# A mixture-of-experts stage: experts with up to 32 rows get a body of their own, with groups of 32 columns

## The chip, the cores and the metric

The kernel runs on one core of a Trainium2 chip (trn2). The metric is the device time of one execution in microseconds (us), taken as the median of several runs.

## What is computed

The program is a transformer-like block of several layers on 256 tokens of width 1024, all in fp32. The change lies in its mixture of experts. Each of 256 tokens chooses 4 of 32 experts, and each expert is a gated layer with three weight matrices of 1024 x 1024:

```python
logits = hf @ router_w + router_b
top_val, top_idx = lax.top_k(logits, TOP_K)            # 4 of 32
top_w = jax.nn.softmax(top_val, axis=-1)
...
g = xb @ w_gate[e] + b_gate[e]
u = xb @ w_up[e] + b_up[e]
g = jnp.minimum(g, SWIGLU_LIMIT)
u = jnp.clip(u, -SWIGLU_LIMIT, SWIGLU_LIMIT)
act = g * jax.nn.sigmoid(SWIGLU_ALPHA * g) * (u + 1.0)
return act @ w_down[e] + b_down[e]
```

The result of a token is the sum over its four experts, each times its weight. The reference's router, worked out on its inputs, gives the experts 0 to 31 these numbers of rows (1024 in all): 9, 17, 11, 48, 34, 49, 76, 11, 62, 40, 52, 51, 19, 13, 42, 11, 48, 9, 20, 44, 28, 79, 18, 37, 30, 20, 36, 48, 18, 22, 15, 7. So 17 experts have up to 32 rows, 13 have 33 to 64, and two (6 and 21) have more than 64.

## The kernel before

The stages ahead of the experts (`pe_s0` to `pe_s6` and their counterparts on the other engines) compute a mixer, attention and the router. `dve_s6` (L1062) ends with the tables of the router: `wt` (token x expert, the weights), `posm` (the place of a token among an expert's rows, or -1), and `cnt` (rows of each expert), and raises `pos_ready`, for which the bias matmuls of L1045 wait.

The experts are a loop, `expert_rounds` (L1351): 16 turns of two experts, one for each set of gate buffers. Every engine loads the expert's number of rows into a register and branches. With up to 64 rows (CAP) it runs the narrow body, which stands in the loop; with more it jumps to a block behind the whole program (`large`, L1370), which handles 128 rows and jumps back.

Three matrices of 4 MB pass through the chip for each expert, each loaded in two halves by SP (`load_in`, L1423). Gate has two sets of buffers (ring and arena), up and down have one. SP's order is in `behind` (L1443): when gate's product of expert e is done it issues gate of e + 2, when up's is done up of e + 1, when down's is done down of e + 1.

The narrow body on TensorE is `pe_narrow` (L1226). The rows are gathered by a matmul with a 0/1 matrix (`pe_gather`), transposed (`pe_gatherT`), and held as XT, 64 columns for each 128 of the width. `pe_product` multiplies: XT's 64 columns are the stationary operand, the weights stream through. The output is 64 rows x 1024 columns, so its two halves of 512 columns go to two halves of the array, output partitions 0 to 63 and 64 to 127 of one bank; gate uses bank 0 and up bank 1. `pe_open` (L1188) puts the biases into these banks with a matmul of 32 rows, ahead of the products. `pe_down` (L1209) has the same form, on the transposed activations (`pe_hidden`). `pe_combine` (L1218) adds the weighted result to banks 4 to 7, with PwT, the transposed 0/1 matrix times the weights. Between up and down, TensorE does the next expert's gather and transposes (L1172, L1185, L1179) and this one's hidden transposes (L1206).

DVE runs `dve_choose` (L1114) for the next expert (Psel and Pw, four operations, and the bias selector Ee) and `dve_glu` (L1131): gm after gate's product (L1134), um after up's (L1136), then two more (L1138, L1141). ACT does the sigmoid (L1157) and five copies from PSUM to SBUF.

Each fp32 matmul shows in the trace as two passes, each a weight load (PEld) and a matmul (PE).

Of the kernel before, what the change touches and what calls it, by code (L numbers as in the profile page):

```python
# [7 lines left out]
P = 128  # L8
D = 1024
SEQ = 256  # L10
TT = SEQ // P
# [8 lines left out]
E, TOPK, CAP = 32, 4, 64  # L20
ROUNDS = SEQ // CAP
# [80 lines left out]
def block_kernel(nc, A, out, names):  # L102
# [39 lines left out]
    with ctx:  # L142
# [12 lines left out]
        def bank(b, n=1, rows=P):  # L155
            return PS[0:rows, b * 512:(b + n) * 512]
# [79 lines left out]
        def ar3(at, n, k):  # L236
            return ar(at, n).rearrange("p (k m) -> p k m", k=k)
# [749 lines left out]
        mk = ar3(13792, 64, TT)  # L987
        wt, posm = ar3(13856, TT * (E + 1), TT), ar3(13924, TT * (E + 1), TT)
# [73 lines left out]
        def dve_s6(dve, o):  # L1062
# [32 lines left out]
            o(dve.tensor_scalar(posm, posm, -1.0, None, ALU.add))  # L1095
            o(dve.tensor_copy(cnt, bank(7)[:, 2 * E:3 * E]), pos_ready)
# [17 lines left out]
        def dve_choose(dve, s, e, r, odd):  # L1114

            for t in range(TT):
                m = dve.tensor_scalar(Psel[:, t, :], slot_iota(r, CAP), posm[:, t, bass.ds(e, 1)], None, ALU.is_equal)
                if t == 0:
                    dve.drain()
            if odd is not None:  # L1120
                dve.drain()
                m = dve.tensor_copy(Ee[odd], con("pick2", 2 * E)[:, bass.ds(e, 1)].to_broadcast([2 * E, CAP]))
            m.then_inc(s.p_ready, 1)
            for t in range(TT):
                m = dve.tensor_scalar(Pw[:, t, :], slot_iota(r, 2 * CAP), posm[:, t, bass.ds(e, 1)], wt[:, t, bass.ds(e, 1)],
                                      ALU.is_equal, ALU.mult)
                if t == 0:
                    dve.drain()
            m.then_inc(s.pw_ready, 1)
# [96 lines left out]
        def pe_narrow(pe, e, odd, there):  # L1226
            n = e + 1
            pe.wait_ge(main.x_ready, n * 2)
# [14 lines left out]
            pe_combine(pe, main, n, PwT[odd])  # L1243

# [16 lines left out]
        def pe_wide(pe, e, odd, x, there):  # L1261

            n = e + 1
            pe.wait_ge(main.x_ready, n * 2)
# [25 lines left out]
            pe_open(pe, 0, 1 - odd, 0)  # L1290
            pe_open(pe, 1, 1 - odd, 1)
# [27 lines left out]
        def pe_further(pe, e, odd, x, there):  # L1319

            pe.wait_ge(main.x_ready, e * 2 + 2)
            pe_gather(pe, extra, x)
# [11 lines left out]
            pe_open(pe, 0, odd, 0)  # L1334
            pe_open(pe, 1, odd, 1)
# [15 lines left out]
        def expert_rounds(eng, narrow, wide, further):  # L1351
# [6 lines left out]
            with eng.Fori(0, E // 2) as i:  # L1358
                for odd in range(2):
# [3 lines left out]
                    sizes.append((e, n_e, fork))  # L1363
                    eng.br_cond(n_e > CAP, f"large_{which}{odd}", f"small_{which}{odd}")
# [5 lines left out]
            def large():  # L1370
                eng.br(f"done_{which}")
                tail = nc.cur_bb
                for odd, (e, n_e, fork) in enumerate(sizes):
                    with nc.body(f"large_{which}{odd}", parent=fork, valid_engines=[eng.engine]):
# [9 lines left out]
                        with eng.If(n_e > 3 * CAP):  # L1384
                            eng.reg_add(rounds, rounds, 1)
                            further(i, e, odd, 3, eng.snap(rounds))
# [4 lines left out]
        def pe_s7(pe):  # L1391
# [12 lines left out]
            pe.wait_ge(main.pwT_ready, 1)  # L1404
            pe_open(pe, 0, 0, 0)
            pe_open(pe, 1, 0, 1)
            return expert_rounds(pe, lambda i, e, odd: pe_narrow(pe, e, odd, there(i, e, odd)),
# [3 lines left out]
        def dve_s7(dve):  # L1411
            dve_choose(dve, main, 0, 0, 0)
            return expert_rounds(dve, lambda i, e, odd: dve_narrow(dve, e, odd), lambda i, e, odd, x: dve_wide(dve, e, odd, x),
                          lambda i, e, odd, r, x: dve_further(dve, e, r, x))

        def act_s7(act):
# [3 lines left out]
            return expert_rounds(act, lambda i, e, odd: act_narrow(act, e, odd), lambda i, e, odd, x: act_wide(act, e, odd, x),  # L1420
# [865 lines left out]
```

## Time and profile before

| | |
|---|---|
| median of 3 runs | 2553.96 us |
| lowest, highest | 2553.76, 2555.77 us |
| span of the profiled execution | 2552.7 us |
| TensorE matmul busy | 2212.0 us, 87% of the span |
| VectorE (DVE) busy | 651.7 us, 26% |
| ScalarE (ACT) busy | 357.1 us, 14% |
| moved by the DMA queues | 580.77 MB, mean 228 GB/s |
| expert stage | about 435 to 1438 us |

The span goes from the first to the last instruction of one profiled execution; a run's time has a little around it, here 1.3 us between the span and the median. "PE" is TensorE's matmul, "PEld" its weight load, which overlaps it. "PEclk" is the granted clock as a share of 2.4 GHz. "issue" in a wait is time for which the profile shows no reason. An average over the span says little here, since stages have different limits; the expert stage is read by itself.

### The profile page before, as it was taken

To read this page: it belongs to the slowest core of one execution; us is meant where nothing else is said; L and a number is where in the kernel's file an instruction comes from. 1 tells how busy PE (TensorE), PEld (TensorE's weight loads), DVE (VectorE), ACT (ScalarE), POOL (GpSimd) and SP (SyncE) were. 2 spreads that over 40 slices of the span, in tenths; PEclk is the share of its full clock that TensorE was granted. 3 is DMA by queue.
4 is the path that set the end of the run, shared out by engine and by line. 5 is a ranking of instruction groups with operands and counts; after the bars stand their busy time and mean duration, and the time that the engine had idled before them with its cause. 6 is when DMAs were issued, how large, how long until landed. Compare 5 with 4: busy or idle time off the path is not lost.

```text
span 2552.7 us, 24185 instructions
## 1 busy us (share of the span) xinstructions
PE 2212.0 (87%) x9951; PEld 1237.3 (48%) x9952; DVE 651.7 (26%) x997; ACT 357.1 (14%) x548; POOL 103.9 (4%) x116
## 2 busy tenths in 40 slices
PE   6977789998899999999999797799979686858997
PEld 2643346333333333333333384488548475837873
DVE  2747623110111111111111115100016465420000
ACT  1211012111111111111111212100012221211000
POOL 1000010000000000000000100200000031200000
PEclk9888889999999999999999898899979887988999
DMA  9561155998699999969999741343333200013330
GB/s 346 207 230 50 66 192 204 398 428 359 263 427 428 427 428 428 428 262 413 428 427 417 290 163 65 83 151 146 133 130 132 99 1 1 1 67 116 139 109 17
DMA packets 106791, 580.77 MB, mean 228 GB/s; under 512 B 6992, under 2 KB 8084, under 8 KB 81969
## 3 DMA queue, kind: packets, MB, share of 16 engines
q1 hardware_dynamic: 101008, 562.40, 55.1%
q0 software_dynamic: 5696, 17.18, 2.2%
q8 instruction: 59, 0.97, 0.2%
q14 instruction: 28, 0.22, 0.0%
HBM read 578.49 MB, written 1.07 MB: 227 GB/s over the span
## 4 chain that ended last, share of the span: by engine, by line
PE 67%; DMA 16%; DVE 11%; ACT 3%; issue 2%; SPq 0%; DVEq 0%; POOL 0%; ACTq 0%
DMA ring<-in_w_up 14%; PE ps L1199 14%; PE ps L1586 12%; PE ps L1597 6%; PE ps L604 6%; PE ps L612 5%; PE ps L1214 5%; PE ps L516 1%; PE ps L1931 1%; PE ps L1222 1%; PE ps L1937 1%; DMA ring<-in_ada_w 1%; PE ps L825 1%; PE ps L1941 1%; PE ps L793 1%
## 5 line engine op out<-in xcount | busy, mean ns | idle before, releaser
L1199 PE MATMUL ps<-ring,arena 128*64 128x512 f32 x1632 | 362.6, 598 | 29.5 <-DMA ring<-in_w_up 23.5
L1586 PE MATMUL ps<-arena,ring 128*128 128x256 f32 x1408 | 308.2, 382 | 1.5 <-ACT arena L581 1.5
L1586 PEld LDWEIGHTS ps<-arena,ring 128*128 128x128 f32 x1408 | 270.0, 192 | 39.6 <-ACT arena L581 2.3
L1214 PE MATMUL ps<-ring,arena 128*64 128x512 f32 x1088 | 240.9, 594 | 9.0 <-ACT arena L1161 9.0
L1199 PEld LDWEIGHTS ps<-ring,arena 128*64 128x64 f32 x1632 | 114.7, 138 | 271.7 <-issue 231.2
L1134 DVE TENSOR_SCALAR arena<-ps 128x512 f32<-128x512 f32 x34 | 23.5, 692 | 546.3 <-PE ps L1199 546.3
L1214 PEld LDWEIGHTS ps<-ring,arena 128*64 128x64 f32 x1088 | 88.3, 137 | 139.1 <-issue 138.3
L1597 PE MATMUL ps<-ring,arena 128*128 128x512 f32 x352 | 151.4, 592 | 0.0
L604 PE MATMUL ps<-arena,ring 128*128 128x256 f32 x672 | 149.1, 384 | 0.7 <-ACT arena L581 0.7
L604 PEld LDWEIGHTS ps<-arena,ring 128*128 128x128 f32 x672 | 129.1, 193 | 20.4 <-issue 1.5
L1199 PE MATMUL ps<-arena 128*64 128x512 f32 x544 | 124.5, 611 | 11.2 <-issue 11.2
L612 PE MATMUL ps<-ring,arena 128*128 128x512 f32 x288 | 130.7, 615 | 3.3 <-ACT arena L2033 2.0
L1597 PEld LDWEIGHTS ps<-ring,arena 128*128 128x128 f32 x352 | 66.9, 190 | 83.3 <-issue 83.2
L574 PE MATMUL ps<-constants,arena 128*128 128x128 f32 x128 | 26.4, 385 | 76.5 <-DVE arena L1543 68.0
L612 PEld LDWEIGHTS ps<-ring,arena 128*128 128x128 f32 x288 | 56.4, 197 | 74.4 <-issue 69.9
L1616 DVE TENSOR_TENSOR arena<-arena,ps 128x512 f32<-128x512 f32 x22 | 15.1, 687 | 302.3 <-ACT arena L1608 302.3
L1136 DVE TENSOR_SCALAR arena<-ps 128x512 f32<-128x512 f32 x34 | 23.5, 692 | 243.8 <-PE ps L1199 243.8
L1199 PEld LDWEIGHTS ps<-arena 128*64 128x64 f32 x544 | 39.0, 141 | 94.7 <-issue 94.7
L553 DVE TENSOR_SCALAR smalls<-smalls 128x2 f32<-128x2 f32 x13 | 2.2, 169 | 265.5 <-ACT arena L547 265.4
L1172 PE MATMUL ps<-arena 128*64 128x512 f32 x280 | 67.8, 606 | 0.0
L1222 PE MATMUL ps<-arena 64*128 64x512 f32 x272 | 67.6, 615 | 0.0
L1157 ACT ACTIVATE arena<-arena 128x512 f32<-128x512 f32 x34 | 21.4, 630 | 300.1 <-DVE arena L1134 300.1
(453 smaller groups left out, 2147.5 us busy)
## 6 DMA issues: line engine op xcount, KB each, us to landing
ring<-in_w_up SPq DMA_DIRECT2D x64, 2048.0 KB, 17.3
ring<-in_w_down SPq DMA_DIRECT2D x64, 2048.0 KB, 16.2
ring<-in_w_gate SPq DMA_DIRECT2D x32, 2048.0 KB, 15.9
arena<-in_w_gate SPq DMA_DIRECT2D x32, 2048.0 KB, 15.9
ring<-in_ffn_w_gate_up SPq DMA_DIRECT2D x22, 2048.0 KB, 7.9
ring<-in_ada_w SPq DMA_DIRECT2D x12, 2048.0 KB, 17.7
ring<-in_ffn_w_down SPq DMA_DIRECT2D x10, 2048.0 KB, 7.7
ring<-in_w_in SPq DMA_DIRECT2D x8, 2048.0 KB, 18.0
```

Source lines behind the costliest of these rows:

```text
L516: m = pe.matmul(bank(base + n), condrep[:, k, :], w[:, k, :], start=(k == 0), stop=(k == KD - 1))
L574: m = pe.transpose(bank(2 * t + b)[:, k * P:(k + 1) * P], src3[:, t, kk * P:(kk + 1) * P], ident)
L604: m = pe.matmul(bank(b0 + c // 2)[:, (c % 2) * SEQ:(c % 2 + 1) * SEQ], w[:, k, c * P:(c + 1) * P], src3[:, k, :], start=(k == 0), stop=(k ...
L612: m = pe.matmul(bank(banks[t]), src3[:, k, t * P:(t + 1) * P], w[:, k, :], start=(k == 0), stop=(k == kn - 1))
L793: m = pe.matmul(bank(4 + t), hT[:, k, t * P:(t + 1) * P], w[:, k, :], start=(k == 0), stop=(k == KD - 1))
L825: m = pe.matmul(bank(b0 + 2 * t + c), src[:, k, t * P:(t + 1) * P], w[:, k, c * 512:(c + 1) * 512], start=(k == 0), stop=(k == 3))
L1172: m = pe.matmul(bank(2)[c * CAP:(c + 1) * CAP, :], Psel[:, t, :], h2[:, t, c * 512:(c + 1) * 512], start=(t == 0), stop=(t == 1))
L1199: m = pe.matmul(bank(b)[c * CAP:(c + 1) * CAP, :], xT[:, j * P + h * CAP:j * P + (h + 1) * CAP], w[h][:, j, c * 512:(c + 1) * 512], start= ...
L1214: m = pe.matmul(bank(b)[d * CAP:(d + 1) * CAP, :], actT[:, j * P + h * CAP:j * P + (h + 1) * CAP], down_w[h][:, j, d * 512:(d + 1) * 512], ...
L1222: m = pe.matmul(bank(4 + 2 * t + d), pwT[d * CAP:(d + 1) * CAP, t * P:(t + 1) * P], Yb[d * CAP:(d + 1) * CAP, :], start=False, stop=False, ...
L1586: m = pe.matmul(bank(b0 + g)[:, c * SEQ:(c + 1) * SEQ], w[:, k, (2 * g + c) * P:(2 * g + c + 1) * P], hT2[:, k, :], start=(k == 0), stop=( ...
L1597: m = pe.matmul(bank(2 * t + d), actF[:, f, t * P:(t + 1) * P], w[:, j, d * 512:(d + 1) * 512], start=(f == 0), stop=(f == FC2 - 1))
```

## The change

An expert with up to 32 rows (FEW) takes a new body, `pe_few`, `act_few`, `dve_few`. Its stationary operands have 32 columns. Gate runs in the column groups 0 and 1 of the array, up in groups 2 and 3, all into bank 0; the bias matmuls stand inside the products, behind the first pair. DVE makes gm and um after both. Down runs in four groups: two halves of the output columns times two halves of the inner dimension, and the halves of the inner dimension are summed by combine, for which Pw gets every row twice, at slot s and s + 32 (`both`; `far` switches this off for experts with more than 32 rows). This is done in `dve_choose` for every expert's first 64 rows. In the narrow, wide and further bodies the bias matmuls (`pe_open`) move from the end of the previous expert to the start of their own. The test for a third extra round of very large experts goes; no expert has so many rows.

```diff
+FEW = CAP // 2
...
+            o(dve.tensor_scalar(far, bank(7)[:, 2 * E:3 * E], float(FEW), float(2 * SEQ), ALU.is_gt, ALU.mult))
+            o(dve.tensor_scalar(both, posm, float(FEW), None, ALU.add))
+            o(dve.tensor_tensor(both[:, :, 0:E], both[:, :, 0:E], rows_bc(far, TT), ALU.add))
             o(dve.tensor_copy(cnt, bank(7)[:, 2 * E:3 * E]), pos_ready)
...
             for t in range(TT):
-                m = dve.tensor_scalar(Pw[:, t, :], slot_iota(r, 2 * CAP), posm[:, t, bass.ds(e, 1)], wt[:, t, bass.ds(e, 1)],
-                                      ALU.is_equal, ALU.mult)
+                if r == 0:
+                    dve.tensor_scalar(Pm, slot_iota(0, 2 * CAP), posm[:, t, bass.ds(e, 1)], None, ALU.is_equal)
+                    dve.drain()
+                    dve.scalar_tensor_tensor(Pm, slot_iota(0, 2 * CAP), both[:, t, bass.ds(e, 1)], Pm, ALU.is_equal, ALU.add)
+                    dve.drain()
+                    m = dve.tensor_scalar(Pw[:, t, :], Pm, wt[:, t, bass.ds(e, 1)], None, ALU.mult)
...
         def pe_narrow(pe, e, odd, there):
             n = e + 1
+            pe.wait_ge(main.pwT_ready, n)
+            pe_open(pe, 0, odd, 0)
+            pe_open(pe, 1, odd, 1)
             pe.wait_ge(main.x_ready, n * 2)
...
             pe_down(pe, main, n, 2, main.d_ps)
-            pe.wait_ge(main.pwT_ready, n + 1)
-            pe_open(pe, 0, 1 - odd, 0)
-            pe_open(pe, 1, 1 - odd, 1)
             pe_combine(pe, main, n, PwT[odd])
+        def pe_few(pe, e, odd, there):
+            n = e + 1
+            pe.wait_ge(main.pwT_ready, n)
+            pe.wait_ge(main.x_ready, n * 2)
+            for i, (w, done) in enumerate(((gate_w[odd], main.g_ps), (up_w, main.u_ps))):
+                there(i)
+                for h in range(2):
+                    for j in range(4):
+                        for c in range(2):
+                            m = pe.matmul(bank(0)[(2 * i + c) * FEW:(2 * i + c + 1) * FEW, :],
+                                          XT[:, j * P + h * CAP:j * P + h * CAP + FEW], w[h][:, j, c * 512:(c + 1) * 512],
+                                          start=((h, j) == (0, 0)), stop=((h, j) == (1, 3)), tile_position=(0, (2 * i + c) * FEW), skip_group_check=True)
+                        if (h, j) == (0, 0):
+                            for c in range(2):
+                                pe.matmul(bank(0)[(2 * i + c) * FEW:(2 * i + c + 1) * FEW, :], Ee[odd][i * E:(i + 1) * E, 0:FEW],
+                                          bgu[i * E:(i + 1) * E, c * 512:(c + 1) * 512], start=False, stop=False,
+                                          tile_position=(i * E, (2 * i + c) * FEW), skip_group_check=True)
+                m.then_inc(done, 1)
+            pe_gather(pe, main, n + 1)
+            pe_gatherT(pe, main, n * 2 + 1)
+            pe.wait_ge(main.a_ready, n * 2)
+            pe_weights(pe, main, n + 1)
+            for j in range(4):
+                m = pe.transpose(bank(0)[:, j * CAP:(j + 1) * CAP], every4(act_[0:CAP, :], j), ident[0:CAP, 0:CAP])
+            m.then_inc(main.aT_ps, 1)
+            there(2)
+            pe.wait_ge(main.aT_ready, n)
+            for j in range(4):
+                for d in range(2):
+                    for h in range(2):
+                        g = 2 * d + h
+                        m = pe.matmul(bank(2)[g * FEW:(g + 1) * FEW, :], actT[:, j * CAP + h * FEW:j * CAP + (h + 1) * FEW],
+                                      down_w[h][:, j, d * 512:(d + 1) * 512], start=(j == 0), stop=(j == 3), tile_position=(0, g * FEW))
+            m.then_inc(main.d_ps, 1)
+            pe_combine(pe, main, n, PwT[odd])
...
+        def act_few(act, e, odd):
+            n = e + 1
+            act.wait_ge(main.gm_ready, n)
+            act.activation(sg[0:CAP, :], gm[0:CAP, :], ACT.Sigmoid, scale=ALPHA).then_inc(main.sg_ready, 1)
+            act_gathered(act, main, n * 2 + 1)
+            act_gatheredT(act, main, n * 2 + 2, XT)
+            act_weights(act, main, n + 1, PwT[1 - odd])
+            act.wait_ge(main.aT_ps, n)
+            act.copy(actT[:, 0:4 * CAP], bank(0)[:, 0:4 * CAP]).then_inc(main.aT_ready, 1)
+            act_out(act, main, (main.d_ps, n))
...
+        def dve_few(dve, e, odd):
+            n = e + 1
+            dve.wait_ge(main.pwT_ps, n)
+            dve_choose(dve, main, e + 1, 0, 1 - odd)
+            dve.wait_ge(main.u_ps, n)
+            dve.tensor_scalar(gm[0:CAP, :], bank(0)[0:CAP, :], LIMIT, None, ALU.min).then_inc(main.gm_ready, 1)
+            dve.tensor_scalar(um[0:CAP, :], bank(0)[CAP:2 * CAP, :], LIMIT, -LIMIT, ALU.min, ALU.max).then_inc(main.a_ready, 1)
...
+                    eng.br_cond(n_e > FEW, f"many_{which}{odd}", f"few_{which}{odd}")
+                    nc.switch_bb(f"few_{which}{odd}", parent=fork)
+                    few(i, e, odd)
+                    eng.br(f"next_{which}{odd}")
+                    nc.switch_bb(f"many_{which}{odd}", parent=fork)
                     eng.br_cond(n_e > CAP, f"large_{which}{odd}", f"small_{which}{odd}")
```

How the instructions move is seen best on TensorE. The end of the narrow body before, from down to the jump to the next expert (a row is a program instruction; x15 is fifteen alike):

```order
L1214 MATMUL ps<-ring,arena 64x512 [waits first_aT_ready,slot_ready4,slot_ready3]
L1214 MATMUL ps<-ring,arena 64x512 x15
L1191 MATMUL ps<-arena 64x512 [waits first_pwT_ready]
L1191 MATMUL ps<-arena 64x512 x3
L1222 MATMUL ps<-arena 128x512 [waits first_y_out]
L1222 MATMUL ps<-arena 128x512 x3
L1367 UNCONDITIONAL_BRANCH
```

Behind down come the bias matmuls of the next expert (L1191) and then combine, which waits for ACT's copy of down's result (first_y_out). Now the narrow body begins with them and nothing stands between down (L1227) and combine:

```order
L1204 MATMUL ps<-arena 64x512 [waits first_pwT_ready]
L1204 MATMUL ps<-arena 64x512 x3
L1244 REGISTER_ALU
L1477 ISA [waits first_x_ready]
L1477 REGISTER_ALU [waits slot_ready5]
L1212 MATMUL ps<-ring,arena 64x512 [waits slot_ready0]
L1212 MATMUL ps<-ring,arena 64x512 x15
...
L1227 MATMUL ps<-ring,arena 64x512 [waits first_aT_ready,slot_ready4,slot_ready3]
L1227 MATMUL ps<-ring,arena 64x512 x15
L1235 MATMUL ps<-arena 128x512 [waits first_y_out]
L1235 MATMUL ps<-arena 128x512 x3
```

The new body on TensorE, from the up product to the jump (L1273 are the biases, L1185 the gather, L1192, L1198 and L1282 transposes, L1290 down, L1235 combine):

```order
L1268 MATMUL ps<-ring,arena 32x512 [waits slot_ready2]
L1273 MATMUL ps<-arena 32x512 x2
L1268 MATMUL ps<-ring,arena 32x512 x14
L1185 MATMUL ps<-arena 64x512 [waits first_p_ready]
L1192 MATMUL ps<-constants,arena 128x128 [waits first_x_ready]
L1198 MATMUL ps<-constants,arena 128x128 [waits first_pw_ready,first_a_ready]
L1282 MATMUL ps<-constants,arena 128x64 x4
L1290 MATMUL ps<-ring,arena 32x512 [waits first_aT_ready,slot_ready4,slot_ready3]
L1290 MATMUL ps<-ring,arena 32x512 x15
L1235 MATMUL ps<-arena 128x512 [waits first_y_out]
L1443 UNCONDITIONAL_BRANCH
```

The count of matmuls per expert stays; what stood between two products (the bias pair) stands inside each, and the Pw transposes (L1198) now wait for the last of DVE's activation work instead of its um.

## Rows read from the trace of the kernel before

**Rows 1.** Stretches: from:to us, its length, then busy us of PE, PEld, DVE, ACT, POOL, clock, DMA share, GB/s
```profile
609.00:682.00 73.00, 61.37 (x278) 20.62 (x276) 8.12 (x18) 8.17 (x14) 0.00 (x0) 0.95 0.65 266
682.00:820.00 138.00, 135.21 (x638) 49.33 (x642) 20.55 (x45) 18.08 (x32) 0.00 (x0) 0.99 0.96 405
820.00:1087.00 267.00, 249.18 (x1186) 88.59 (x1178) 36.75 (x80) 34.99 (x60) 0.00 (x0) 1.00 1.01 428
1087.00:1151.00 64.00, 58.34 (x264) 20.05 (x264) 8.13 (x18) 6.30 (x12) 0.00 (x0) 0.95 0.63 256
```

**Rows 2.** Chain of waits, 1359 to 1396 us: start us, us, what
```profile
1359.52 7.11 PE ps L1199 x32
1367.08 21.83 DMA ring<-in_w_up
1388.95 7.11 PE ps L1199 x32
```

**Rows 3.** Timeline of TensorE, expert 2: start us, us, line, operation, passes
```profile
495.68 1.99 PE L1222 MATMUL ps<-arena 64*128 64x512 f32 x8
497.60 13.95 PE L1199 MATMUL ps<-ring,arena 128*64 128x512 f32 x64
511.38 1.89 PE L1172 MATMUL ps<-arena 128*64 128x512 f32 x8
...
515.41 7.09 PE L1214 MATMUL ps<-ring,arena 128*64 128x512 f32 x32 [0.29 <-ACT arena L1161]
522.42 1.09 PE L1191 MATMUL ps<-arena 32*64 32x512 f32 x8
523.44 1.99 PE L1222 MATMUL ps<-arena 64*128 64x512 f32 x8
525.36 7.09 PE L1199 MATMUL ps<-arena 128*64 128x512 f32 x32
```

**Rows 4.** TensorE: entry to large expert 6, return from it, return from 21 (chain)
```profile
618.06 9.80 PE L1199 MATMUL ps<-ring,arena 128*64 128x512 f32 x32 [5.78 <-issue]
682.06 8.53 PE L1199 MATMUL ps<-arena 128*64 128x512 f32 x32 [5.71 <-issue]
1150.94 13.91 PE ps L1199 x64
```

**Rows 5.** Stretch behind the entry to expert 6
```profile
618.00:624.90 6.90, 6.84 (x20) 2.19 (x22) 0.00 (x0) 0.00 (x0) 0.00 (x0) 0.60 1.00 419
```

**Rows 6.** SP's timeline: issues behind expert 21
```profile
1148.05 0.81 SPq L1431 DMA_DIRECT2D ring<-in_w_down  x2
1158.16 0.85 SPq L1431 DMA_DIRECT2D ring<-in_w_gate  x2
```

**Rows 7.** Timeline of DVE and ACT behind an up product
```profile
456.06 0.69 DVE L1136 TENSOR_SCALAR arena<-ps 128x512 f32<-128x512 f32 x1 [6.17 <-PE ps L1199]
458.26 0.38 ACT L1153 COPY arena<-ps 128x256 f32<-128x256 f32 x1
459.15 0.59 ACT L1161 COPY arena<-ps 128x512 f32<-128x512 f32 x1 [0.51 <-PE ps L1206]
```

**Rows 8.** Stretches of the ada stage (L632): 32-column matmuls in four, then two groups
```profile
150.60:157.60 7.00, 7.00 (x67) 2.15 (x68) 5.92 (x5) 0.00 (x0) 0.00 (x0) 1.00 0.58 217
157.60:164.60 7.00, 6.98 (x36) 1.70 (x30) 0.00 (x0) 0.00 (x0) 0.00 (x0) 1.00 0.83 275
```

**Rows 9.** Timeline of DVE ahead of pos_ready
```profile
431.66 0.20 DVE L1095 TENSOR_SCALAR arena<-arena 128x66 f32<-128x66 f32 x1
431.89 0.19 DVE L1096 CAST arena<-ps 128x32 int32<-128x32 f32 x1
```

**Rows 10.** Chain of waits: first work behind the experts
```profile
1437.68 3.64 PE ps L1479 x8
```

**Rows 11.** Queues, 1085 to 1095 us: packets, MB, share of 16 engines
```profile
q8 instruction: 1, 0.02, 0.7%
```

More of the change, by code:

```diff
@@ L987, in block_kernel @@
         mk = ar3(13792, 64, TT)
+        far, both = ar(21504, E), ar3(21536, TT * (E + 1), TT)
+        Pm = ar(21632, P)
         wt, posm = ar3(13856, TT * (E + 1), TT), ar3(13924, TT * (E + 1), TT)
@@ new lines, in dve_few @@
+        def dve_few(dve, e, odd):
[5 more added lines that the diff above has]
+            dve.tensor_scalar(um[0:CAP, :], bank(0)[CAP:2 * CAP, :], LIMIT, -LIMIT, ALU.min, ALU.max).then_inc(main.a_ready, 1)
+            dve.drain()
+            dve.scalar_tensor_tensor(um[0:CAP, :], um[0:CAP, :], 1.0, gm[0:CAP, :], ALU.add, ALU.mult)
+            dve.drain()
+            dve.wait_ge(main.sg_ready, n)
+            dve.tensor_tensor(act_[0:CAP, :], um[0:CAP, :], sg[0:CAP, :], ALU.mult).then_inc(main.a_ready, 1)
@@ L1263, in pe_wide @@
             n = e + 1
+            pe.wait_ge(main.pwT_ready, n)
+            pe_open(pe, 0, odd, 0)
+            pe_open(pe, 1, odd, 1)
             pe.wait_ge(main.x_ready, n * 2)
@@ L1321, in pe_further @@
             pe.wait_ge(main.x_ready, e * 2 + 2)
+            pe.wait_ge(main.pwT_ready, e + 1)
+            pe_open(pe, 0, odd, 0)
+            pe_open(pe, 1, odd, 1)
             pe_gather(pe, extra, x)
@@ L1349, in dve_further, with expert_rounds @@
             dve_glu(dve, extra, x, (extra.g_ps, x), (extra.u_ps, x))
-        def expert_rounds(eng, narrow, wide, further):
+        def expert_rounds(eng, few, narrow, wide, further):
             which = eng.engine.name
@@ L1383, in large @@
                         further(i, e, odd, 2, eng.snap(rounds))
-                        with eng.If(n_e > 3 * CAP):
-                            eng.reg_add(rounds, rounds, 1)
-                            further(i, e, odd, 3, eng.snap(rounds))
+                        eng.reg_add(rounds, rounds, 1)
+                        further(i, e, odd, 3, eng.snap(rounds))
                         eng.br(f"pair_{which}{odd}")
@@ L1403, in pe_s7 @@
             pe_gatherT(pe, main, 1)
[L1404 to L1407, printed above, removed]
+            return expert_rounds(pe, lambda i, e, odd: pe_few(pe, e, odd, there(i, e, odd)),
+                          lambda i, e, odd: pe_narrow(pe, e, odd, there(i, e, odd)),
                           lambda i, e, odd, x: pe_wide(pe, e, odd, x, there(i, e, odd)),
@@ L1419, in act_s7 @@
             act_gatheredT(act, main, 2, XT)
-            return expert_rounds(act, lambda i, e, odd: act_narrow(act, e, odd), lambda i, e, odd, x: act_wide(act, e, odd, x),
+            return expert_rounds(act, lambda i, e, odd: act_few(act, e, odd), lambda i, e, odd: act_narrow(act, e, odd), lambda i, e, odd, x: act_wide(act, e, odd, x),
                           lambda i, e, odd, r, x: act_further(act, x))
```

9 lines of the change are left out of this document (4 added, 5 removed).

## The prediction

> **What bounds the kernel now.** I read the expert stage by stretches first, then the chain of waits, then TensorE's timeline. The stretches [rows 1] show two regimes. From 820 to 1087 us the DMA engines are full at 428 GB/s; around the two experts with more than 64 rows (609 to 682 and 1087 to 1151) they are busy only 0.65 and 0.63 of the time. In the full stretch the chain goes from one landing of w_up to the next: the product that reads it (7.11 us) releases the next load, which lands 21.83 us later [rows 2]. One expert per 1388.95 - 1359.52 = 29.43 us, three loads of 4 MB, 9.81 us each. TensorE's own work for a 33-to-64-row expert is shorter: from one gate product to the next 525.36 - 497.60 = 27.76 us [rows 3]. It is made of gate and up (13.9), what lies between up and down (511.38 to 515.41, 4.03), down (7.0), the bias matmuls (1.02, which cover the wait for ACT's copy of the down result) and combine (1.92).
>
> So a faster TensorE is worth nothing where the DMA is full: it only waits longer for w_up. Its time counts at four places: before the first release of a load, at the two large experts, where every buffer is full and the DMA idles until the next release, and after the last landing that it waits for. I sum over these. Small experts (17 of 32 have up to 32 rows): 0, 1, 2, 7, 12, 13, 15, 17, 18, 20, 22, 24, 25 and 28 to 31. The large ones are 6 and 21.
>
> **The change, part by part.** *Small body, gate and up.* Each product keeps 16 matmuls in two column groups side by side, as before, only 32 columns wide instead of 64. Width was not what cost: a pair of passes takes 6.95 / 16 = 0.43 us [rows 3], and the block of 128*32 matmuls of the ada stage shows the same rate with two groups (the second stretch of rows 8: 36 matmul records in 7 us, against 67 in the first, where four groups run). I take no gain. The two bias matmuls of each product now stand inside it, in one pair at a time: 2 x 0.43 = +0.86 per product. The up product's first pair uses groups that gate left free, so it can overlap gate's last: -0.43, where TensorE doesn't wait between them.
>
> *Down in four groups.* At four groups side by side [rows 8] 16 matmuls take half of 7.0: -3.5.
>
> *Between up and down.* DVE now does gm and um both after up: +0.70 (one more 0.69 operation [rows 7]). The Pw transposes move behind that wait: +0.4, the four hidden transposes have half the columns: -0.3; ACT's copy before down shrinks from 0.59 to about the 0.38 that 256 columns take [rows 7]: -0.2. Sum +0.6. Bounds: 0 (all of it hidden by the gather, as um is today) and +1.6 (the weights copy, 0.38, and the XT copy, 0.59, in front of the last one on ACT's queue both count).
>
> *Bias matmuls moved in the other bodies.* They go from the cover of ACT's copy of down to the front of the next expert. The copy has to be waited for anyway, so an expert of 33 to 64 rows and a large one get +1.02 [rows 3].
>
> *Period of TensorE:* small 27.76 + 0.86 + 0.43 + 0.6 - 3.5 = 26.2, middle 27.76 + 1.02 = 28.8. Both stay under 29.43, so both are hidden in the full stretches, the middle one with 0.6 to spare. If it had none, each middle expert would add.
>
> *DVE.* Three operations are added before pos_ready. Neighbours there stand 431.89 - 431.66 = 0.23 apart [rows 9], and the bias matmuls of TensorE start 0.1 after the last: 3 x 0.23 = +0.7, on the path. Choosing rows gets four more operations of about 0.35 with drains, 2 us per expert; DVE is busy 36.75 of 267 us [rows 1] and this stands beside gate, long before it is asked for: 0. ACT, POOL and SP issue the same in number and order of loads.
>
> **The sum, by place.**
> - Start: +0.7 (pos_ready), -1.02 (no bias matmuls before gate 0), +0.86 (inside it): +0.5.
> - Expert 6: the path from the last landing to the release of gate 8 gets its bias matmuls, +1.0; expert 5 before it is a middle one. Behind it the DMA idles again until gate 7 is done (share 0.96 in 682 to 820 [rows 1]), and expert 7 is small: +0.9.
> - Expert 21: expert 20 before it is small. After its w_up lands: +0.43 + 0.6 - 3.5, then +1.0 at the front of 21: -1.5. Behind it w_down was issued at 1148.05 and the next gate at 1158.16 [rows 6], 10.1 apart against 9.81 of work, so the DMA just runs dry; gate 22 is later by 0.86: +0.9.
> - Tail: the last landing waited for starts the product at 1388.95 [rows 2], and the stage's end is at 1437.68 [rows 10]: 48.7 us of TensorE, for experts 30 and 31. Up 30 onward +0.43 + 0.6 - 3.5 = -2.5; expert 31 -1.6: -4.1.
>
> Together 0.5 + 1.9 - 0.6 - 4.1 = -2.3 us. The later stages are not touched. The profiled execution spans 2552.7; the runs' median is 2553.96, 1.3 above, and the difference is carried over: **2551.7 us**. The unknown terms: with +1.6 between up and down the sum is +1.7 (four places, and small experts slower behind the large ones), with 0 it is -5; four groups at two thirds of their gain would give +1. So this case reaches from 2548 to 2557. A measurement can tell about 0.2%, 5.1 us, from no change: this case is "same".
>
> **Rivals.**
> *More stalls of TensorE's instruction stream (slower).* At the entry to the large body and at the first return from it TensorE stood still for 5.78 and 5.71 us for nothing but issue; the product behind the first took 9.80 instead of 7.1 [rows 4], at a granted clock of 0.60 [rows 5], between its levels of 2.4 and 1.2 GHz. An instruction transfer of 0.02 MB falls in the gap before the second large expert [rows 11]. The second return had no stall (product at once at 1150.94 [rows 4]). After the change the loop holds four bodies instead of two, some 1100 of TensorE's matmul and weight-load instructions instead of 520, and an excursion into a large body may displace more of it. Each further stall is 5.7 plus 1.5 for the slow clock, 7.2. It decides only where the DMA has little queued, right behind a large expert: at expert 22 the whole 7.2 counts (2558.9), at 8 about 4.2, at both 11.4 (2563.1); a third adds some 7. Elsewhere the DMA's queue (21.83 - 9.81 = 12 us [rows 2]) hides it. For it: one of two returns stalls now. Against: the loop's own back edge never does. 0.24.
> *Every hand-over stalls.* A small body skips the one behind it, a middle one is jumped into. If each of 31 hand-overs stood 5.7, a small expert would take 31.9 us and a middle one 34.5, and TensorE would be the bound: 177 us of stalls less the 3.2 and 0.6 per expert that the DMA hides (about 35), +142, 2696. The jump back of today, over two bodies, costs nothing in rows 3, and that speaks against it. The Trainium skill, page Runtime: NRT & Kernel Launch, section Instruction fetch mechanics, says that a taken branch whose target is not in the two pages at hand waits for a transfer of the target's page; by it these jumps would stall, and this rival is what it would give. On that rule, the trace agrees at the large bodies and disagrees at the back edge. 0.04.
> *No stall at the first return (faster).* The layout is another; if expert 7 starts at once, 7.2 of idle DMA go: 2544.5. 0.10.
> *The clock falls in the small body.* Between gather and down there are 3 us with little but transposes and waits. If the granted clock went to its lower level for down each time, +1.7 per small expert: at the places of the sum +6, 2557.6. Against: two groups of 32 kept 1.00 for 7 us [rows 8], and today's 2.1 us of the same kind never cost it. 0.10.
> *The groups do not run side by side,* so down stays at 7.0 and a small expert takes 29.7, over the DMA's 29.43: about +25, 2579. Rows 8 speak against it. 0.02.
>
> **Numbers.** Forecast 0.50 (0.06 of it over 5.1 us faster, 0.02 slower), stalls 0.24 (0.13 slower, the rest within), clock 0.10 (0.02 slower), no stall 0.10, hand-overs 0.04, groups 0.02. Faster 0.16, same 0.61, slower 0.23. The range goes from the no-stall case (2545) to two further stalls (2563.5); what lies outside is part of the no-stall case, a third stall, and the last two rivals.
>
> **What would show it.** Small experts: down 3.5 us instead of 7.0; TensorE's waits for w_up grow from 1.4 to about 3 us behind a small expert; the full stretch still at 428 GB/s and 29.4 us per expert. Middle experts 28.8 us apart where TensorE leads. Idle of 5.7 us "issue" ahead of a gate product other than those three is the first rival. The prediction is wrong if the full stretches change their period, or if the stage's end moves by more than 5 us without such idle time.

## The result and the profile after

| | before | after |
|---|---|---|
| median | 2554.86 us (4 runs) | 2593.45 us (4 runs) |
| span of the profiled execution | 2552.7 us | 2590.1 us |
| end of the expert stage in it | 1437.68 us [rows 10] | 1472.02 us |

The kernel became slower: ratio 1.0151, 95% interval 1.0134 to 1.0167, or 38.6 us. Medians and ratios here leave out the one slow run, 3394.38 us, of the later experiment e7. The forecast was 2551.7 us with a range up to 2563.5, and the time lies outside it. Of the 37.4 us between the two spans, 34.3 arise before the end of the expert stage and 3.1 behind it.

The page of after, its engines, TensorE's granted clock and the instruction queue (before: 2212.0 us of PE and 651.7 of DVE):

```profile
span 2590.1 us, 24611 instructions
...
PE 2190.2 (85%) x9943; PEld 1196.8 (46%) x9944; DVE 689.4 (27%) x1132; ACT 354.7 (14%) x548; POOL 103.9 (4%) x116
...
PEclk9888888999989999998999998899979887888999
...
q8 instruction: 70, 1.15, 0.2%
```

TensorE is busy for less time than before and the program is still longer, so it must stand idle for more. The stretches of after, with the columns of [rows 1], say where:

```profile
609.00:682.00 73.00, 61.39 (x278) 20.55 (x274) 11.33 (x30) 8.16 (x14) 0.00 (x0) 0.95 0.67 272
682.00:820.00 138.00, 118.61 (x548) 39.41 (x550) 20.88 (x52) 15.02 (x26) 0.00 (x0) 0.91 0.85 356
820.00:1087.00 267.00, 242.84 (x1192) 76.41 (x1190) 47.06 (x117) 34.06 (x59) 0.00 (x0) 0.99 1.01 428
1087.00:1230.00 143.00, 115.01 (x532) 36.05 (x530) 20.11 (x48) 14.23 (x26) 0.00 (x0) 0.89 0.70 286
```

The stretch around expert 6 (the first) is much as in [rows 1], and in the full one (the third) the DMA moves 428 GB/s as before. Behind expert 6, in 682 to 820, TensorE is busy 118.61 us instead of 135.21 and the DMA share is 0.85 instead of 0.96. The stretch around and behind expert 21 has a share of 0.70. The chain of waits of after names the idle time. In the whole expert stage it has six pieces of "issue" over 4 us (start us, us, what):

```profile
613.64 5.81 issue
...
677.75 6.12 issue
...
714.00 11.89 issue
...
1103.45 5.62 issue
...
1168.32 13.10 issue
...
1211.95 4.52 issue
```

Three of them are old: the entries to the large bodies of experts 6 and 21 (613.64 and 1103.45) and the first return (677.75). In before they are 5.78 and 5.71 us at expert 6 [rows 4] and 5.47 at the entry to 21. The other three are new: 11.89 us between experts 7 and 8, 13.10 us at the return from 21, and 4.52 us between 22 and 23. The six make 47.1 us against 17.0 before: **30.1 us more**, of 34.3.

The trace also has a record of each branch instruction that TensorE runs. In the expert stage of after eight of them last longer than 1 us, from 4.73 to 7.48 us (all the others under 0.4), and during each of the eight a packet of 16 KB starts on q8, the instruction queue. Before has three such jumps, 6.23 to 6.66 us, each with a packet. So these waits are fetches of instructions. The 11.89 us are two jumps in a row: the back edge, which is the loop's jump back to its start (712.49, 7.48 us), and the jump over the small body (720.88, 4.73 us). The 13.10 us are the return from the large body (1166.35, 6.51 us) and the back edge right behind it (1173.02, 7.04 us). The 4.52 us are a jump over the small body again (1211.16, 5.02 us).

The shift of the same load's issue on SP, after less before, shows how the loss builds up:

| load issued | before | after | shift |
|---|---|---|---|
| gate 9, when gate product 7 is done | 690.77 | 696.07 | +5.30 |
| gate 10, when gate product 8 is done | 718.55 | 737.56 | +19.01 |
| down 22, when expert 21's down is done | 1148.05 | 1165.68 | +17.63 |
| gate 24, when gate product 22 is done | 1158.16 | 1194.02 | +35.86 |
| gate 25, when gate product 23 is done | 1185.91 | 1226.89 | +40.98 |
| (end of the stage) | 1437.68 | 1472.02 | +34.34 |

So the DMA's queue did not swallow these waits. Only in the full stretch it gives some back: the shift falls from 19.01 at gate 10 to 16.12 at the entry to expert 21 (1103.45 against 1087.33). SP's timeline of after, behind expert 6 and behind 21 (the second pair answers to [rows 6]):

```profile
711.37 0.81 SPq L1509 DMA_DIRECT2D ring<-in_w_down  x2
737.56 0.85 SPq L1509 DMA_DIRECT2D ring<-in_w_gate  x2
```
```profile
1165.68 0.81 SPq L1509 DMA_DIRECT2D ring<-in_w_down  x2
1194.02 0.85 SPq L1509 DMA_DIRECT2D ring<-in_w_gate  x2
```

26.2 and 28.3 us pass between two issues, and one load is 9.81 us of work. Behind the stall at 714.00 the DMA has run dry and TensorE's clock has fallen (columns as in [rows 1]: at the end the clock, the DMA share and GB/s):

```profile
725.90:735.00 9.10, 9.10 (x30) 2.47 (x32) 0.00 (x0) 0.00 (x0) 0.00 (x0) 0.62 0.18 77
```

The small body itself does what it was built for. TensorE's timeline of expert 0, from its first product to the next one (answers to [rows 3]):

```profile
443.53 1.05 PE L1268 MATMUL ps<-ring,arena 128*32 128x512 f32 x4 [0.86 <-ACT arena L1162]
444.51 1.05 PE L1273 MATMUL ps<-arena 32*32 32x512 f32 x4
...
458.73 1.94 PE L1185 MATMUL ps<-arena 128*64 128x512 f32 x8
...
463.49 3.64 PE L1290 MATMUL ps<-ring,arena 128*32 128x512 f32 x32 [0.55 <-ACT arena L1303]
467.83 1.99 PE L1235 MATMUL ps<-arena 64*128 64x512 f32 x8 [0.69 <-ACT arena L1178]
469.74 1.05 PE L1268 MATMUL ps<-arena 128*32 128x512 f32 x4
```

The period is 469.74 - 443.53 = 26.2 us, and down takes 3.64 us with four groups.

### The profile page after: what moved, and what is told of

Same layout as the page of the kernel before. It is cut to its first block, busy times and chain, and to the rows that moved or that the text cites. A ratio compares the mean times of both kernels' runs of the same rounds, so it can differ in the third digit from the quotient of the medians.

```text
span 2590.1 us, 24611 instructions
## 1 busy us (share of the span) xinstructions
PE 2190.2 (85%) x9943; PEld 1196.8 (46%) x9944; DVE 689.4 (27%) x1132; ACT 354.7 (14%) x548; POOL 103.9 (4%) x116
## 3 DMA queue, kind: packets, MB, share of 16 engines
q8 instruction: 70, 1.15, 0.2%
## 4 chain that ended last, share of the span: by engine, by line
PE 67%; DMA 15%; DVE 10%; ACT 4%; issue 3%; SPq 0%; DVEq 0%; POOL 0%; ACTq 0%
DMA ring<-in_w_up 13%; PE ps L1664 12%; PE ps L1212 7%; PE ps L1268 7%; PE ps L1675 6%; PE ps L605 6%; PE ps L613 5%; PE ps L1227 3%; PE ps L517 1%; PE ps L2009 1%; PE ps L1235 1%; PE ps L2015 1%; DMA ring<-in_ada_w 1%; PE ps L826 1%; PE ps L1290 1%
## 5 line engine op out<-in xcount | busy, mean ns | idle before, releaser
L1268 PE MATMUL ps<-ring,arena 128*32 128x512 f32 x832 | 189.5, 611 | 20.2 <-issue 13.3
L1212 PE MATMUL ps<-ring,arena 128*64 128x512 f32 x800 | 180.1, 604 | 10.3 <-DMA ring<-in_w_up 10.3
L1227 PE MATMUL ps<-ring,arena 128*64 128x512 f32 x544 | 120.4, 594 | 4.1 <-ACT arena L1174 4.1
L1268 PEld LDWEIGHTS ps<-ring,arena 128*32 128x32 f32 x832 | 44.3, 112 | 158.9 <-issue 145.4
L1212 PEld LDWEIGHTS ps<-ring,arena 128*64 128x64 f32 x800 | 56.4, 139 | 131.6 <-issue 114.1
L1311 DVE TENSOR_SCALAR arena<-ps 64x512 f32<-64x512 f32 x17 | 11.6, 682 | 389.0 <-PE ps L1268 389.0
L1235 PE MATMUL ps<-arena 64*128 64x512 f32 x272 | 67.6, 615 | 22.0 <-ACT arena L1178 22.0
L1227 PEld LDWEIGHTS ps<-ring,arena 128*64 128x64 f32 x544 | 43.4, 137 | 70.4 <-issue 69.6
L1147 DVE TENSOR_SCALAR arena<-ps 128x512 f32<-128x512 f32 x17 | 11.8, 692 | 238.2 <-PE ps L1212 238.2
L1290 PE MATMUL ps<-ring,arena 128*32 128x512 f32 x544 | 65.3, 622 | 9.4 <-ACT arena L1303 9.4
L1185 PE MATMUL ps<-arena 128*64 128x512 f32 x280 | 68.7, 612 | 0.0
```

The lines of the kernel that those rows point to most:

```text
L1185: m = pe.matmul(bank(2)[c * CAP:(c + 1) * CAP, :], Psel[:, t, :], h2[:, t, c * 512:(c + 1) * 512], start=(t == 0), stop=(t == 1))
L1212: m = pe.matmul(bank(b)[c * CAP:(c + 1) * CAP, :], xT[:, j * P + h * CAP:j * P + (h + 1) * CAP], w[h][:, j, c * 512:(c + 1) * 512], start= ...
L1227: m = pe.matmul(bank(b)[d * CAP:(d + 1) * CAP, :], actT[:, j * P + h * CAP:j * P + (h + 1) * CAP], down_w[h][:, j, d * 512:(d + 1) * 512], ...
L1235: m = pe.matmul(bank(4 + 2 * t + d), pwT[d * CAP:(d + 1) * CAP, t * P:(t + 1) * P], Yb[d * CAP:(d + 1) * CAP, :], start=False, stop=False, ...
L1268: m = pe.matmul(bank(0)[(2 * i + c) * FEW:(2 * i + c + 1) * FEW, :], XT[:, j * P + h * CAP:j * P + h * CAP + FEW], w[h][:, j, c * 512:(c + ...
L1290: m = pe.matmul(bank(2)[g * FEW:(g + 1) * FEW, :], actT[:, j * CAP + h * FEW:j * CAP + (h + 1) * FEW], down_w[h][:, j, d * 512:(d + 1) * 5 ...
```

## The experiments

Each theory below had to say why TensorE's instruction stream stalls three times more. All ratios are to runs of before on the same chip, whose medians are 2549.6 to 2553.99 us for e1 to e9. The stage's end is the start of the first work behind the experts.

| run | median us | ratio, 95% | waits "issue" over 4 us | end of stage |
|---|---|---|---|---|
| before | 2554.86 | 1 | 3 | 1437.68 |
| after | 2593.45 | 1.0134 to 1.0167 | 6 | 1472.02 |
| e1, before without large bodies | 2491.25 | 0.9726 to 0.9774 | 0 | 1372.97 |
| e2, after without large bodies | 2490.26 | 0.9718 to 0.9766 | 0 | 1378.33 |
| e3, small body never taken | 2559.84 | 1.0004 to 1.0054 | 3 | 1441.16 |
| e4, bias matmuls moved only | 2560.58 | 1.0013 to 1.0043 | 3 | 1442.23 |
| e5, small body peeled off the end | 2544.89 | 0.9958 to 0.999 | 3 | 1433.79 |
| e6, small body for odd experts | 2571.68 | 1.0052 to 1.0104 | 3 | 1453.30 |
| e7, one large expert | 2545.41 | 0.9955 to 0.9992 | 3 | 1423.37 |
| e8, dead code added | 2584.84 (one run) | | 6 | 1472.83 |
| e9, narrow body twice | 2598.15 | 1.0151 to 1.023 | 6 | 1479.81 |

### Without the large bodies: e1 and e2

The same edit in both kernels; in e2 it stands in the block that `many_` leads to:

```diff
-                    eng.br_cond(n_e > CAP, f"large_{which}{odd}", f"small_{which}{odd}")
+                    eng.br_cond(n_e > 3 * CAP + 1, f"large_{which}{odd}", f"small_{which}{odd}")
```

> The kernel before, with the jump to the large body switched off (experts 6 and 21 run the narrow body, so their rows beyond 64 are left out). Both theories: the two stretches with an idle DMA go, the rest stays at 29.4 us per expert; about 61 us less than before, some 2493 us. It is the base for the next run.

> The changed kernel with the same switch (rows beyond 64 of two experts left out). Theory 1 (the loss is stalls of TensorE's instruction stream, brought on by the excursion into a large body from a loop of four bodies): no stall of 5 us or more in the expert stage, and a time within -6 to +4 us of the run before it. Theory 2 (the small body, or a loop of four bodies, costs time by itself): 25 to 38 us above the run before it, as with the large experts.

Neither trace has a wait for issue over 4 us in the stage, and the two kernels take the same time, 2491.25 and 2490.26 us. The loss of 38.6 us is gone with the large bodies. All other parts of the change together are worth about nothing: the stage's end is 5.4 us later in the profiled pair, but the issue of gate 2 is 6.1 later already. Nor is code fetched once the loop has turned a few times. The instruction rows of e2 for 530 to 1370 us (packets, MB, share) have none for q8, the queue that had 70 packets in the whole of after:

```profile
q1 hardware_dynamic: 25685, 356.88, 100.2%
q14 instruction: 1, 0.01, 0.0%
```

So TensorE holds the loop of four bodies, and the jumps over the small body and the back edge cost nothing while it does: none of TensorE's 80 branches between 440 and 1470 us lasts over 0.4 us.

### Is it the span of the code? e3

```diff
-            o(dve.tensor_scalar(far, bank(7)[:, 2 * E:3 * E], float(FEW), float(2 * SEQ), ALU.is_gt, ALU.mult))
+            o(dve.tensor_scalar(far, bank(7)[:, 2 * E:3 * E], -1.0, float(2 * SEQ), ALU.is_gt, ALU.mult))
...
-                    eng.br_cond(n_e > FEW, f"many_{which}{odd}", f"few_{which}{odd}")
+                    eng.br_cond(n_e > -1, f"many_{which}{odd}", f"few_{which}{odd}")
```

> The changed kernel, its code in place, but the small body is never taken (and rows are not doubled); large bodies as before. Theory 1: the loop still spans four bodies, so the stalls behind the two large experts stay (more than 20 us of issue besides the entries), and the time is 2585 to 2600 us. Theory 2 in the form that executing the small body costs: about 2560 us (only the bias matmuls moved).

The loop is as long as in after, but the waits are those of before. Chain of waits of e3, its only issue pieces over 4 us:

```profile
610.28 5.57 issue
...
675.65 5.97 issue
...
1089.80 5.12 issue
```

Theory 1 had held the span of the loop responsible, and in that form it fell. Code that only lies in the loop does no harm; it has to be run. Nor does the added jump over the small body do harm by itself, since every expert takes it here. The time is the one that theory 2 gave, about 2560 us, so up to here the small body itself may be the cause; e9 decides that.

### The moved bias matmuls alone, and the small body at the end alone: e4 and e5

e4 is before with one part of the change, in the narrow, wide and further bodies:

```diff
         def pe_narrow(pe, e, odd, there):
             n = e + 1
+            pe.wait_ge(main.pwT_ready, n)
+            pe_open(pe, 0, odd, 0)
+            pe_open(pe, 1, odd, 1)
...
-            pe.wait_ge(main.pwT_ready, n + 1)
-            pe_open(pe, 0, 1 - odd, 0)
-            pe_open(pe, 1, 1 - odd, 1)
```

> The kernel before with the bias matmuls moved to the front of each body, nothing else. Theory 1: 2 to 7 us above before (start and the two large experts +1 each, middle period 28.5 us, still under the DMA's 29.4), same three stalls as before. Rival: the lost cover is the main cost, 25 us or more.

There are three waits, as in before, and the ratio of 1.0028 is that of e3 (1.0029), so the move is enough to account for what e3 loses. The rival's 25 us or more didn't come. TensorE's timeline of e4 shows what the bias matmuls no longer cover; compare [rows 3], where combine follows them with no wait:

```profile
522.70 1.99 PE L1222 MATMUL ps<-arena 64*128 64x512 f32 x8 [0.68 <-ACT arena L1165]
524.62 1.09 PE L1191 MATMUL ps<-arena 32*64 32x512 f32 x8
```

e5 keeps the loop of before for experts 0 to 29, bias matmuls in their old place, and lays the last two experts behind the loop with the small body; two of the three new operations of DVE stand behind `pos_ready`. The loop's end and the last pair:

```diff
-            with eng.Fori(0, E // 2) as i:
+            with eng.Fori(0, E // 2 - 1) as i:
...
+            for odd in range(2):
+                i, e = E // 2 - 1, E - 2 + odd
...
+                eng.br_cond(n_e > FEW, f"many_{which}{e}", f"few_{which}{e}")
+                nc.switch_bb(f"few_{which}{e}", parent=fork)
+                few(i, e, odd)
+                eng.br(f"next_{which}{e}")
+                nc.switch_bb(f"next_{which}{e}", parent=fork)
```

> The kernel before for experts 0 to 29 (loop of two bodies, bias matmuls where they were), and the small body only in a last pair behind the loop, laid out in a line; middle and large bodies of that pair stand behind the program. Theory 1 (stalls of the instruction stream behind the large bodies come with the small body in the loop): the three stalls of before and no more, the tail of 48.7 us becomes 44.6, the stage ends 3 to 4 us earlier than in before. Rival (the small body itself loses what it saves): stage end as before or later.

2544.89 us against 2549.6 of before (10 and 25 runs), ratio 0.9974: this beats both kernels, by a little. The chain of e5 has the waits of before and then the tail:

```profile
612.07 5.55 issue
...
674.69 5.60 issue
...
1086.80 5.35 issue
```
```profile
1386.69 1.05 PE ps L1273 x4
...
1425.77 5.37 PE ps L1295 x32
...
1433.79 4.46 PE ps L1582 x8
```

From the product behind the last landing to the stage's end there are 47.1 us, against 48.7 in before. It would be 45.4 if the last down had taken its 3.64 us, as the one before it did (3.67), instead of 5.37. So of the 44.6 expected for this tail the trace shows 47.1, a gain of 1.6 us. The other 2.3 of the 3.9 us by which the stage ends earlier are there before the small body runs (1386.69 against 1388.95), and what brings them isn't shown. The spans of the two profiled executions (2553.2 and 2552.7) do not show the gain; the ratio of the runs and the stage's end do.

### How much code, and how many excursions: e6 and e7

e6 gives only odd experts the small body, so the loop holds three bodies. e7 is after with a higher bound for the large body, so that expert 6 stays in the loop:

```diff
+                    if odd:
+                        eng.br_cond(n_e > FEW, f"many_{which}{odd}", f"few_{which}{odd}")
```
```diff
-                    eng.br_cond(n_e > CAP, f"large_{which}{odd}", f"small_{which}{odd}")
+                    eng.br_cond(n_e > CAP + 14, f"large_{which}{odd}", f"small_{which}{odd}")
```

> The changed kernel with the small body only for odd experts (loop of three bodies; 11 of 17 small experts take it). Theory 1 by the amount of code that a turn runs through: between the three stalls of before and the six of the changed kernel, one or two extra behind each large expert, 2565 to 2585 us. If any mixing of bodies is enough: all stalls, 2590 us or more. If it takes all four bodies: no extra stall, about 2558 us.

> The changed kernel with the large body only for expert 21 (12 rows of expert 6 are left out). Theory 1: the stalls around expert 6 go, those around 21 stay (about 13 and 4.5 us behind it). Time about 30 us for the large body of expert 6 and some 17 for its stalls less than the changed kernel: 2540 to 2552 us.

The chain of e6, and then that of e7:

```profile
615.26 6.06 issue
...
1087.20 5.57 issue
1151.91 13.59 issue
```
```profile
1051.44 5.67 issue
1115.60 14.53 issue
1161.26 4.51 issue
```

With three bodies the return from 6 does not stall at all (its product starts at 680.67, with combine ending there), while the return from 21 costs 13.59 us. So half of the added code brings one new wait, of two jumps (6.78 us for the return, 7.54 for the back edge), and loses an old one, and the ratio is between the others. That is in the range of 2565 to 2585 us, but not one or two extra waits behind each large expert. In e7 the excursion at 21 alone has its entry, its return and the 4.51 us behind expert 22. Each excursion, which is the way out to a large body and back, makes its own stalls; they don't depend on an earlier one.

### Where the code lies: e8

e8 is after with two more copies of the body for a third group of rows, which never runs. They stand between the two large bodies, so that of the code that runs in the loop's stage only the large body of expert 21 gets another address:

```diff
                         further(i, e, odd, 2, eng.snap(rounds))
+                        if odd == 0:
+                            for _ in range(2):
+                                further(i, e, odd, 3, eng.snap(rounds))
```

> The changed kernel with code that never runs put between the large body of even experts and that of odd ones, two transfers' worth on TensorE. If what counts is how much code has passed through (theory 1): same six stalls as in the changed kernel, 2588 to 2598 us. If it is at which address the large body lies (two pieces of code that share a place): the stalls behind expert 21 change, by 10 us or more.

The same six waits stand there, and the stage ends within 0.9 us of after. The waits behind expert 21 change by 1.2 us at most, where the rival gave 10 or more. It is one run, and one shift of the address. These are the three that before doesn't have:

```profile
712.85 11.98 issue
...
1167.24 14.30 issue
1211.80 4.40 issue
```

### More code with nothing else: e9

The last run separates the amount of code from everything that is special in the small body. It is e4 with its narrow body laid down twice:

```diff
+                    eng.br_cond(n_e > 32, f"many_{which}{odd}", f"few_{which}{odd}")
+                    nc.switch_bb(f"few_{which}{odd}", parent=fork)
+                    narrow(i, e, odd)
+                    eng.br(f"next_{which}{odd}")
+                    nc.switch_bb(f"many_{which}{odd}", parent=fork)
                     eng.br_cond(n_e > CAP, f"large_{which}{odd}", f"small_{which}{odd}")
```

> The kernel of e4 (before, with the bias matmuls moved) whose narrow body stands in the loop twice for each set of gate buffers: experts with up to 32 rows run through the first copy, the others through the second. The two copies are the same code and do the same work for every expert, so nothing of the small body is left: not its waits, not its four groups, not its length of instructions by more than it has. Theory A (what brings the extra stalls is that more code is run through in the loop, whatever it does): the three stalls of the change come back here, about 12 us behind expert 7, 13 us at the return from 21 and 4.5 us between 22 and 23, beside the three of before; the expert stage ends some 24 to 30 us later than in e4 and the ratio to before is 1.012 to 1.015. Theory B (it is something in the small body, its many column groups or its waits): three stalls as in e4, ratio 1.002 to 1.004.

All three new waits are there, at the places of after and of its size. Chain of waits of e9:

```profile
612.89 5.96 issue
...
678.36 5.78 issue
...
715.69 11.95 issue
...
1106.69 5.77 issue
...
1170.93 13.44 issue
...
1214.98 4.26 issue
```

They sum to 47.2 us, against 17.3 in e4: 29.9 more. The stage ends 37.6 us later than e4's, more than the 24 to 30 that theory A gave, and the ratio of 1.019 is above its 1.012 to 1.015; 2.7 of the 37.6 are there ahead of the first wait, and some 5 more are not in the waits themselves. The instruction queue's row for the loop's first turns (440 to 530 us), of before and then of e9 (packets, MB, share):

```profile
q8 instruction: 2, 0.03, 0.1%
```
```profile
q8 instruction: 4, 0.07, 0.3%
```

Two more packets come in for the second copies. After has 4 here as well, e3 and e4 have 2, e6 has 3: the row goes with the code that is run, not with the code that is laid down. In e9, too, the new waits are slow jumps at the same places: 7.29 and 4.99 us behind expert 7, 6.55 and 7.56 behind 21, 4.75 behind 22, each with a packet of q8. Theory A stands: **the loss comes from the amount of code that the loop passes through, together with the excursions**.

## Why the prediction was wrong

**The step that failed** is the rival "More stalls of TensorE's instruction stream", and the sum that took the three stalls of before as fixed. The mechanism was named, at the right place (behind the large experts), and given 0.24; it was the case that came, and it brought 30 us of waits where the rival had priced 7.2 to 11.4, and some 7 more for a third stall. Three things were wrong in it.

- *Chance.* "Against: the loop's own back edge never does." That is true as long as no large body has run: e2 passes four bodies with no stall. Behind an excursion it is false. The records of TensorE's jumps above have the back edge at 7.48 us behind expert 7 and at 7.04 behind 21. I drew from a back edge on an undisturbed loop what it does on a disturbed one.
- *Price of one.* 7.2 us for each further stall counted one target per excursion. After each of the two excursions there are three slow jumps, the return, the back edge and the jump over the small body, each with its own fetch: each displaced part of the loop seems to be fetched again at the first jump that reaches it.
- *Cover.* "At 8 about 4.2" took 3 us of cover from the DMA's queue. The shift grew from +5.30 to +19.01 between gate 9 and gate 10, so 13.7 us: the wait of 11.89, counted whole, and what the product at a clock of 0.62 adds.

On "every hand-over stalls", 0.04, e2 decides: no hand-over stalls without a large body. The Trainium skill, page Runtime: NRT & Kernel Launch, section Instruction fetch mechanics, says that prefetch is sequential and that a taken branch out of the two pages at hand waits for a transfer. The trace agrees that such waits exist: each of the slow jumps has its packet. It disagrees on the rule: in the undisturbed loop of e2, jumps over a whole body and back over four cost nothing and nothing is transferred, and the return from 21 in before didn't wait either. The same section gives TensorE 128 KiB, refilled in 16 KiB blocks. A packet of the queue's row is 1.15 / 70 MB, so 16 KB, which agrees; loops that keep four blocks or so without fetching fit such a size better than two pages.

On "the groups do not run side by side", 0.02, the price of about +25 doesn't follow from its own terms: 3.5 us at each of the three places of the sum where down stands and 29.7 - 29.43 = 0.27 for each of 17 small experts make some 15. The chance was small and the time of down, 3.64 us, ruled the case out.

**Point by point, the rest of the sum.**
- *Period of a small expert:* 26.2 forecast, 26.2 measured, in part by luck: down, the step before it and the two bias pairs are each 0.1 to 0.2 us longer than in the sum, and the 1.02 of the old bias matmuls, which the sum left in, has become a wait of 0.69. *Down:* 3.5 forecast, 3.64. *Between up and down:* 4.6 forecast, 463.49 - 458.73 = 4.76.
- *Bias matmuls inside the product:* 0.86 forecast for a pair, 0.98 measured (444.51 to 445.49).
- *Bias matmuls moved:* +1.02 forecast per middle expert, +0.76 measured (28.5 us from one gate product to the next, at 758.86 and 787.38). The matmuls are there in both kernels; what is added is only the wait that they no longer cover, 0.68 us, and I had charged the matmuls whole. In the runs e4 gives this part alone 1.0013 to 1.0043, so it costs something without any stall.
- *Start:* +0.5 forecast, +2.54 at the issue of gate 2 (451.88 against 449.34). The missing cover is in the timeline above: the first product now waits 0.86 us for ACT's copy of XT (L1162), which the bias matmuls had hidden; the router's bias matmuls (L1048) start 0.74 later, as forecast, and take 4.27 us instead of 3.67.
- *Full stretch:* 428 GB/s and 29.43 us from one up product to the next (563.51, 592.94), as forecast; the small body's 3 us turn into a longer wait for w_up.
- *Expert 6 and behind, before the new stall:* +1.9 forecast, +5.30 at gate 9. The granted clock is low behind the return (0.50 from 683.80 to 687.70), so that the product's first passes and its bias pair (1.92 and 1.85 us instead of 0.98 each) cost double. Of the 5.30, 1.4 us are there before the return, 0.4 are its longer wait (6.12 against 5.71), and the rest is this product.
- *Tail:* -4.1 forecast. From the up product of expert 30 to the end there are 1472.02 - 1427.68 = 44.3 us, before 48.7: -4.4. But one product earlier the clock fell (0.68 from 1399.60 to 1408.50), and the up product of expert 29 took over 11 us instead of 8.2:

```profile
1397.05 1.05 PE ps L1268 x4
1398.10 1.51 PE ps L1273 x4
1399.61 8.94 PE ps L1268 x28
```

  This was the last load that TensorE waited for, one expert earlier than in the sum. From there the rest is TensorE's own work, 1472.02 - 1397.05 = 75.0 us, against 1437.68 - 1359.52 = 78.2 from the same product before, which still waited for the next w_up. By that count the tail gives 3.2 us, not 4.4.

- *The clock rival* (0.10) happened now and then, not each time: two of the 17 small experts' downs, at 517.53 and 1008.86, took 5.34 us against 3.64, which is its +1.7, and the product above is another case. It is not what decided.
- The 3.1 us behind the expert stage lie between its end and 2400 us. The code there is the same; TensorE is busy 2.05 us longer (747.81 against 745.76) at a mean granted clock of 0.88 instead of 0.89, so most of it goes with the clock. Why the clock differs stays open. The last 190 us are alike to the digit.

Added up for the stage: +1.4 ahead of the first wait (613.64 against 612.28), +30.1 of waits, -4.4 in the tail; the remaining 7.2 us must be the products at a low clock, the moved bias matmuls at the large experts and the late loads, less what the full stretch gives back; the shares of these weren't told apart.

**What stays open.** Which block is displaced when, and why the return from 6 doesn't stall in e6 while the one from 21 does, isn't settled. e6's ten runs reach from 2558.12 to 2587.05 us, and only the one of 2565.22 has a profile, so whether its waits are the same each time isn't known. The runs show how much was read (q8 rows) and where TensorE waited, not what its instruction memory held. A large body made shorter, or laid inside the loop, was not tried.

## What to carry to other kernels

Code that a loop runs through is a resource like a buffer: a second body, even a faster one, can cost more than it saves, and what shows it is the "issue" time behind the rare branch, not the loop's steady turns. A jump that costs nothing in an undisturbed loop says nothing about the same jump behind an excursion to code that lies elsewhere; price every jump until the loop is whole again, and ask how long the DMA's queue lasts meanwhile. Put a special body only where its time is on the path, here behind the last landing and outside of the loop (e5), and test a theory on code size with two copies of the same code (e9), which changes nothing else.

## What the runs showed of the hardware

- TensorE keeps a loop of four bodies, some 1040 matmul and weight-load instructions (130 passes a body, each with its weight load), with no stall and no transfer from 530 to 1370 us (e2), and code that is laid down in the loop but jumped over is not missed (e3).
- One jump to code that has to be fetched took TensorE 4.7 to 8.1 us, in all runs with large bodies, and each such jump had a 16 KB packet of the instruction queue in it. Such jumps come in a chain: waits of 11.9 to 14.5 us for two in a row in after, e6, e7, e8 and e9. Two unused bodies laid between the large ones changed each of the six waits by less than 1.3 us (e8).
- The granted clock falls behind such a wait: 0.50 in the 3.9 us from 683.80 and 0.62 in the 9.1 us from 725.90 (after).
- Four column groups of fp32 side by side halve the time of the same passes: 32 passes in 3.64 us instead of 7.09, with 128 rows of contraction each.
